# A hybrid decoder trunk: the compression of one attention branch as 16 joint products for keys and values

## The reference

```python
nc = S // CMP_STRIDE - 1                       # 256 // 16 - 1 = 15
def compress(t, pe, w):                        # t: (B, S, 64), pe: (32, 64), w: (32 * 64, 64)
    ch = t.reshape(B, S // CMP_STRIDE, CMP_STRIDE, d)
    blk = jnp.concatenate([ch[:, :-1], ch[:, 1:]], axis=2)
    return ((blk + pe).reshape(B, nc, CMP_LEN * d) @ w).astype(F32)
kc = compress(keys[:, :, 0], cmp_pe[0], w_cmp[0])
vc = compress(vals[:, :, 0], cmp_pe[1], w_cmp[1])
```

## Time and profile before

| | |
|---|---|
| median of 3 timed runs | 1626.65 us (1624.82 to 1626.75) |
| profiled execution | 1623.64 us, span 1622.0 us |
| TensorE busy | 1543.1 us (95%) |
| VectorE busy | 1250.4 us (77%) |
| ScalarE busy | 1015.1 us (63%) |
| mean granted TensorE clock | 0.961 of full |
| mixer of layer 0, loop and transposes | about 80 to 156 us |
| mixer of layer 1, loop and transposes | about 503 to 581 us |
| experts | from about 625 us to the end |

### The profile page before, as it was taken

How to read it: one execution, slowest core, us unless ns; L and a number is a source line. 1 busy time by engine, 2 the same in 40 slices (tenths; PEclk the granted TensorE clock), 3 DMA queues, 4 the chain that set the end, 5 groups by cost and what they waited for, 6 DMA issues and landing times.

```text
span 1622.0 us, 20490 instructions
## 1 busy us (share of the span) xinstructions
PE 1543.1 (95%) x7534; PEld 1293.3 (80%) x7534; DVE 1250.4 (77%) x1279; ACT 1015.1 (63%) x920; POOL 77.8 (5%) x106
## 2 busy tenths in 40 slices
PE   7989899999799995999999999999999999999996
PEld 5978688888698874888888888888888888888884
DVE  6777654444558666889988988988988988988985
ACT  6456443444355442778778778778778778777763
POOL 2101000000000011000000000000000000000000
PEclk9988999999899695999999999999999999999998
DMA  9701555556350032999999999999999999999991
GB/s 299 230 1 38 188 196 190 182 182 196 105 191 27 1 104 92 381 393 350 384 393 349 387 393 346 394 394 343 395 395 343 393 396 342 393 397 352 393 397 40
DMA packets 189879, 444.69 MB, mean 274 GB/s; under 512 B 9633, under 2 KB 15918, under 8 KB 189822
## 3 DMA queue, kind: packets, MB, share of 16 engines
q1 hardware_dynamic: 185214, 427.82, 71.8%
q0 software_dynamic: 4608, 16.10, 3.9%
HBM read 436.03 MB, written 7.86 MB: 274 GB/s over the span
## 4 chain that ended last, share of the span: by engine, by line
PE 91%; DVE 5%; issue 2%; ACT 1%; DMA 0%; POOL 0%; SPq 0%; ACTq 0%; POOLq 0%; DVEq 0%
PE bank L408 26%; PE bank L409 25%; PE bank L407 25%; PE bank L535 2%; PE bank L462 2%; PE bank L538 1%; PE bank L674 1%; PE bank L656 1%; PE bank L633 1%; DVE work L1737 1%; PE bank L684 1%; DVE hT L1557 1%; PE bank L648 1%; PE bank L863 0%; PE bank L387 0%
## 5 line engine op out<-in xcount | busy, mean ns | idle before, releaser
L1602 DVE TENSOR_TENSOR w_lo<-ring,w_hi 128x2048 fp32r<-128x2048 f32 x375 | 853.5, 2291 | 193.6 <-ACT w_hi L1211 192.2
L1211 ACT ACTIVATE w_hi<-ring 128x2048 fp32r<-128x2048 f32 x375 | 716.1, 1915 | 222.0 <-PE bank L407 221.9
L408 PE MATMUL bank<-w_hi,xT_hi 128*128 128x512 f32 x896 | 354.5, 396 | 5.8 <-ACT w_hi L1211 5.8
L409 PE MATMUL bank<-w_hi,xT_lo 128*128 128x512 f32 x896 | 350.5, 391 | 0.0
L407 PE MATMUL bank<-w_lo,xT_hi 128*128 128x512 f32 x896 | 240.6, 390 | 0.0
L408 PE MATMUL bank<-w_hi,hidT_hi 128*128 128x512 f32 x560 | 220.5, 394 | 1.6 <-DVE hidT_lo L1609 1.6
L409 PE MATMUL bank<-w_hi,hidT_lo 128*128 128x512 f32 x560 | 218.3, 390 | 0.0
L408 PEld LDWEIGHTS bank<-w_hi,xT_hi 128*128 128x128 f32 x896 | 168.9, 188 | 40.2 <-ACT w_hi L1211 6.2
L407 PEld LDWEIGHTS bank<-w_lo,xT_hi 128*128 128x128 f32 x896 | 168.7, 188 | 35.7
L409 PEld LDWEIGHTS bank<-w_hi,xT_lo 128*128 128x128 f32 x896 | 169.0, 189 | 34.0
L408 PE MATMUL bank<-w_hi,hT_hi 128*128 128x512 f32 (+2 forms) x384 | 149.8, 393 | 9.9 <-DVE hT_lo L1562 9.8
(11 more groups left out here) (335 smaller groups left out, 1395.0 us busy)
## 6 DMA issues: line engine op xcount, KB each, us to landing
ring<-in_moe_w_gate_dram SPq DMA_DIRECT2D x112, 1024.0 KB, 9.9
ring<-in_moe_w_up_dram SPq DMA_DIRECT2D x112, 1024.0 KB, 9.3
ring<-in_moe_w_down_dram SPq DMA_DIRECT2D x112, 1024.0 KB, 9.5
ring<-in_ffn_w_gate_dram SPq DMA_DIRECT2D x14, 1024.0 KB, 5.2
ring<-in_ffn_w_up_dram SPq DMA_DIRECT2D x14, 1024.0 KB, 5.1
ring<-in_ffn_w_down_dram SPq DMA_DIRECT2D x14, 1024.0 KB, 4.9
ring<-in_w_in_dram SPq DMA_DIRECT2D x12, 1024.0 KB, 5.2
ring<-in_w_out_dram SPq DMA_DIRECT2D x8, 1024.0 KB, 7.4
```

The lines of the kernel that those rows point to most:

```text
L408: pe.matmul(o, x_hi, w, start=start, stop=False)
L409: return pe.matmul(o, x_lo, w, start=False, stop=False)
L1211: act.activation(w_hi[:, (base + at) % SPLIT, :], ring[:, i, :], ACT.Copy).then_inc(hi_ready, 1)
L1602: dve.tensor_tensor(w_lo[:, v, :], ring[:, (base + at) % RING, :], w_hi[:, v, :].bitcast(F32), ALU.subtract).then_inc(lo_ready, 1)
```

## The change

The 32 positions of a block are split into two halves of 16. The raw keys and values are turned twice, into partitions 0 to 63 and again into 64 to 127, side by side as `kvT2`. Partitions 0 to 63 then serve positions 0 to 15 and partitions 64 to 127 positions 16 to 31. The lower copy is a transpose as before, the upper one a plain product with the identity. The weights of keys and values lie beside each other, 128 columns in 128 rows, and 16 products of 128 rows, 128 columns and 30 streamed columns (15 blocks of keys, 15 of values) give both results at once. Of the result, keys by keys' columns (rows 0 to 63) and values by values' columns (rows 64 to 127) are used. Values come out turned and are transposed once more (`turn_values`).

```diff
-        w_cmp = sb("w_cmp", [P, CLEN, HD])
-        pe_row = sb("pe_row", [CLEN, L, P])
-        pe_t = sb("pe_t", [P, L, CLEN])
+        w_cmp = sb("w_cmp", [P, CLEN // 2, 2 * HD])
+        pe_t = sb("pe_t", [P, L, 2, CLEN // 2])
...
+        pe_row = work[0:CLEN // 2, out_at + TB * GW:out_at + 2 * TB * GW].rearrange("p (l c q) -> p l c q", l=L, c=2)
...
-        N_PROW = 12
+        N_PROW = 13
...
             for l in range(L):
-                mm = pe.transpose(b[:, 2 * P + l * CLEN:2 * P + (l + 1) * CLEN], pe_row[:, l, :],
-                                  ident[0:CLEN, 0:CLEN])
+                for c in range(2):
+                    at = 2 * P + (2 * l + c) * (CLEN // 2)
+                    mm = pe.transpose(b[:, at:at + CLEN // 2], pe_row[:, l, c, :], ident[0:CLEN // 2, 0:CLEN // 2])
...
-                    pe.wait_ge(mixw_in, 64 * (l + 1))
+                    pe.wait_ge(mixw_in, 96 * (l + 1))
...
                 b = bank(1)
-                for tb in range(TB):
-                    pe.transpose(b[:, tb * P:(tb + 1) * P], utok[:, tb, KV0:KV0 + 2 * HD], ident[:, :])
-                for tb in range(TB):
-                    mm = pe.transpose(b[0:HD, S + tb * P:S + (tb + 1) * P],
-                                      utok[:, tb, KV0 + 2 * HD:KV0 + 3 * HD], ident[:, :])
+                for c in range(2):
+                    for tb in range(TB):
+                        v = utok[:, tb, KV0 + c * HD:KV0 + (c + 1) * HD]
+                        t = slice(c * S + tb * P, c * S + (tb + 1) * P)
+                        pe.transpose(b[0:HD, t], v, ident[:, :])
+                        mm = pe.matmul(b[HD:P, t], v, ident[:, :], start=True, stop=True)
                 give(mm, 1)
                 b = bank(1)
-                for tb in range(TB):
-                    mm = pe.transpose(b[0:HD, tb * P:(tb + 1) * P],
-                                      utok[:, tb, KV0 + 4 * HD:KV0 + 5 * HD], ident[:, :])
+                for i in range(2):
+                    for tb in range(TB):
+                        mm = pe.transpose(b[0:HD, i * S + tb * P:i * S + (tb + 1) * P],
+                                          utok[:, tb, KV0 + (2 + 2 * i) * HD:KV0 + (3 + 2 * i) * HD], ident[:, :])
...
-                def compressed_keys():
+                def compress():
 
                     pe.wait_ge(cin_ready, l + 1)
                     b = bank(0)
-                    for j in range(CLEN):
-                        mm = pe.matmul(b[0:HD, 0:NC], w_cmp[0:HD, j, :], cin[0:HD, j, :], start=(j == 0),
-                                       stop=(j == CLEN - 1))
+                    for j in range(CLEN // 2):
+                        mm = pe.matmul(b[:, 0:2 * NC], w_cmp[:, j, :], cin[:, j, :, :].rearrange("p c n -> p (c n)"),
+                                       start=(j == 0), stop=(j == CLEN // 2 - 1))
                     give(mm, 0)
+                    mark["cmp", l] = gave[0]
 
-                def compressed_values():
+                def turn_values():
 
+                    pe.wait_ge(cmp_ready, 2 * l + 1)
                     b = bank(0)
-                    for j in range(CLEN):
-                        mm = pe.matmul(b[0:NC, 0:HD], cin[HD:P, j, :], w_cmp[HD:P, j, :], start=(j == 0),
-                                       stop=(j == CLEN - 1))
-                    give(mm, 0)
-                    mark["cmp", l] = gave[0]
+                    give(pe.transpose(b[0:NC, 0:HD], kcv[HD:P, 1, :], ident[HD:P, HD:P]), 0)
...
                     if n == 3:
                         ssd_sums()
-                        compressed_keys()
+                        compress()
...
                     if n == 6:
-                        compressed_values()
+                        turn_values()
                         ssd_products()
...
-            sp.dma_start(pe_row[:, :, :].rearrange("r l (i d) -> r (l i) d", i=2),
-                         nsa_cmp_pe.rearrange("l i r d -> r (l i) d")).then_inc(prow_in, 16)
+            for half in range(2):
+                sp.dma_start(pe_row[:, :, :, half * HD:(half + 1) * HD].rearrange("r l c d -> r (l c) d"),
+                             nsa_cmp_pe[:, :, half * (CLEN // 2):(half + 1) * (CLEN // 2), :]
+                             .rearrange("l c r d -> r (l c) d")).then_inc(prow_in, 16)
...
-                for i in range(2):
-                    pool.dma_start(w_cmp[i * HD:(i + 1) * HD, :, :],
-                                   nsa_w_cmp[l, i].rearrange("(j d) e -> d j e", d=HD)).then_inc(mixw_in, 16)
+                for c in range(2):
+                    for half in range(2):
+                        pool.dma_start(w_cmp[half * HD:(half + 1) * HD, :, c * HD:(c + 1) * HD],
+                                       nsa_w_cmp[l, c, half * (CLEN // 2) * HD:(half + 1) * (CLEN // 2) * HD]
+                                       .rearrange("(j d) e -> d j e", d=HD)).then_inc(mixw_in, 16)
...
                 b = filled()
-                act.activation(kvcT[:, :], b[:, 0:S], ACT.Copy)
-                act.activation(ksT[0:HD, :], b[0:HD, S:2 * S], ACT.Copy).then_inc(act_took, 1)
+                act.activation(kvT2[:, :, :], b[:, :].rearrange("p (c t) -> p c t", c=2), ACT.Copy)\
+                    .then_inc(act_took, 1)
                 b = filled()
-                act.activation(kwT[0:HD, :], b[0:HD, 0:S], ACT.Copy).then_inc(act_took, 1)
+                act.activation(kswT[0:HD, :, :], b[0:HD, :].rearrange("p (c t) -> p c t", c=2), ACT.Copy)\
+                    .then_inc(act_took, 1)
...
-                for i in range(2):
-                    src = kvcT[:, 16 * i:16 * i + 16 * NC].rearrange("p (n j) -> p j n", j=16)
-                    pos = pe_t[:, l, 16 * i:16 * i + 16].unsqueeze(2).broadcast_to([P, 16, NC])
-                    ins = dve.tensor_tensor(cin[:, 16 * i:16 * i + 16, :], src, pos, ALU.add)
-                    if i == 0:
+                for half in range(2):
+                    r = slice(half * HD, (half + 1) * HD)
+                    at = half * (CLEN // 2)
+                    src = kvT2[r, :, at:at + 16 * NC].rearrange("p c (n j) -> p j c n", j=16)
+                    pos = pe_t[r, l, :, :].rearrange("p c j -> p j c").unsqueeze(3)\
+                        .broadcast_to([HD, CLEN // 2, 2, NC])
+                    ins = dve.tensor_tensor(cin[r, :, :, :], src, pos, ALU.add)
+                    if half == 0:
...
-                        take_bank(dve.tensor_copy(kcT[0:HD, :], b[0:HD, 0:NC]))
+                        take_bank(dve.tensor_copy(kcv[:, :, :], b[:, 0:2 * NC].rearrange("p (c n) -> p c n", c=2)))
```

More of the change, by code:

```diff
@@ L186, in trunk @@
                 at(b3, MLA_H, S), take(MLA_H, S),
-                at(b4, NH, S), take(S), take(S), take(S), take(NC), take(HD), take(TB, SSD_H),
-                at(b5, CLEN, NC), take(TB, GW), take(TB, GW), take(SSD_H, P),
+                at(b4, NH, S), take(2, S), take(2, NC), take(HD), take(TB, SSD_H),
+                at(b5, CLEN // 2, 2, NC), take(TB, GW), take(TB, GW), take(SSD_H, P), at(used[0] - SSD_H * P, 2, S),
                 at(b6, SSD_H, S)))
@@ L495, in _ @@
                 p = BASE_MIX[l]
-                (qtok, kcat, vtok, xb, xbc, qT, kT, nqT, kvcT, ksT, kwT, kcT, vc, nacs, cin, xtok, xdt, dec1,
+                (qtok, kcat, vtok, xb, xbc, qT, kT, nqT, kswT, kcv, vc, nacs, cin, xtok, xdt, dec1, kvT2,
                  dec0) = mix_bufs[l]
@@ L629, in scores @@
                             q, k = {"mla": (qT[0:QK, h, t0:t1], kT[0:QK, h, 0:nk]),
-                                    "cmp": (nqT[0:HD, h, t0:t1], kcT[0:HD, :]),
-                                    "sel": (nqT[0:HD, h, t0:t1], ksT[0:HD, 0:nk]),
-                                    "win": (nqT[0:HD, h, t0:t1], kwT[0:HD, 0:nk])}[br]
+                                    "cmp": (nqT[0:HD, h, t0:t1], kcv[0:HD, 0, :]),
+                                    "sel": (nqT[0:HD, h, t0:t1], kswT[0:HD, 0, 0:nk]),
+                                    "win": (nqT[0:HD, h, t0:t1], kswT[0:HD, 1, 0:nk])}[br]
                             mm = pe.matmul(b[:, i * nk:(i + 1) * nk], q, k, start=True, stop=True)
@@ L1534, in _ @@
             link(dve.tensor_copy(par[:, :, :], b[:, 0:2 * P].rearrange("p (l c) -> p l c", l=L)))
-            take_bank(dve.tensor_copy(pe_t[:, :, :], b[:, 2 * P:2 * P + L * CLEN].rearrange("p (l c) -> p l c", l=L)))
+            take_bank(dve.tensor_copy(pe_t[:, :, :, :], b[:, 2 * P:2 * P + L * CLEN]
+                                      .rearrange("p (l c j) -> p l c j", l=L, c=2)))
             def lam_start():
```

6 lines of the change are left out of this document (3 added, 3 removed).

## The result

The changed kernel takes 1640.7 us (median of 4 runs, 1638.8 to 1641.4) against 1626.1 us, a ratio of 1.0089 (95% interval 1.0072 to 1.0107). It is 14.6 us slower, and 15.7 us over the forecast. Its profiled execution took 1641.41 us, span 1639.6, granted clock 0.947 where before had 0.961.

A forecast was written before the change was run, and what follows sets the result against it. TensorE was taken as the bound, the chain running through it for 91% of the span. Terms 0 (joint products) - 3.75 + 1.6 + 0.5 = -1.65 us, so 1626.65 becomes 1625.0 us; range 1619.5 to 1630.5.

The forecast's parts named there:

- The value products' term: Mixers: value products leave TensorE, 3.67 us a layer; 2.1 us in layer 0 and 1.65 in layer 1 arrive, -3.75 together.
- Rival D: Between value transpose and squares (L760) the clock falls; 1628.5 us for one layer, 1632 for both; chance 0.17.
- The transposes: Before first scores: bank takes 1.3 us, ScalarE waits 0.64 and copies 0.17 longer; +0.81 us a layer, +1.6 in all.
- (C): New transpose bank: each change of output half drains, 1.3 us a layer, 1627.6 us; transposes' bound +2.1; chance 0.09.
- The dense FFN and the experts are the same instructions: Outside the mixers: whatever a mixer gains or loses moves dense FFN and experts as a block.
- Joint products: Mixers' key products: 32 records at 111 ns, 3.6 us, against 64 at 58 ns, 3.7 us; taken as 0.
- VectorE's additions: Building the products' input: double the elements, 2.3 us for 1.16, hidden by the wait before the scores; cost 0.
- its wait at the outputs: VectorE's 1.05 us wait at L1939 in each layer's mixer goes when the value products go.
- GpSimd's four loads: Compression weights: four DMAs where two took 2.19 us, 1.1 us more, at most 2.2; hidden, cost 0.
- The start: Kernel start: one more DMA issue, +0.30 us, and four narrow transposes for two, +0.36; +0.5 taken, bounds 0.3 and 0.7.
- The offset: Profiled execution of 1623.64 us, 3.0 under the median 1626.65; a difference worked out from it was put on the median.

The follow-up runs named there:

- Grouping: Changed kernel with its four lower-half transposes first, then its four upper-half products: 1631.7 us, ratio 1.0038.
- The transposes alone: Kernel before with four pairs of an upper-half product and a transpose added in each layer: 1633.6 us, ratio 1.0047.
- The three later traces with before's mixers: Kernel before with 44 tiny TensorE products (1632.8 us), with 56 (1626.8 us), and with its overflow loop inside one condition (1623.2 us).
- the padded kernel at 224: Kernel before with 56 tiny TensorE products in the waits around 640 us, final code at position 224 of a 256-instruction block: 1626.8 us, ratio 1.0010.
- the four attempts to hold it: Eight dense products added: changed kernel at n=6, 1639.8 us; also halves grouped, 1633.5; also at n=4, 1637.3; kernel before at n=4, 1648.9.

## Why the prediction was wrong

1. **The value products' term, -3.75 us, is the step that failed in the mixers.** Its working took the clock of the trace before as given and only moved work inside it. Removing them alone costs 6.7 us. Rival D named the mechanism, the stretch between the value transpose and the squares, and had 0.17. Its layer-0 form is in the trace after (0.50 from 143 to 149). In layer 1 more happened than it said: low from 549 to 580, where before was low from 540 to 557 only and high to 575.
2. **The transposes, +1.6 us, are mis-sized.** They took 2.27 us for the bank and +1.96 us a layer to the first scores, 3.9 in all, which is (C)'s 2.1 a layer. Grouping shows 0.13 us for each change. The Trainium skill's rule on drains (TensorEngine Tiling (Array Packing), Key Properties), as the prediction applied it, made this free; the measurement decides against that reading. Whether the half or the change between transpose and plain product drains was not separated. ScalarE waited 1.62 us, not 0.64. The transposes alone, 2.3 us later a layer, also took clock: 7.3 us in all.
3. **What the sum has no term for: the end, 7.6 us.** "The dense FFN and the experts are the same instructions" is true and did not help: TensorE's program ahead of them is 336 instructions shorter, and the jumps behind them cost by place. The experts themselves took the same time (961.1 and 961.3 us).
4. **Joint products, 0.** Right by themselves (111 ns a record), 0.5 to 4 us dearer in the kernel.
5. **VectorE's additions** took 1.98 us (forecast 2.3), and it still waited 1.00 us for the scores behind them: hidden, as forecast. In layer 0 its wait at the outputs (L1939 of before) went as forecast; in layer 1 it is 2.76 us where the earlier trace rows has 1.05, since TensorE is slow there.
6. **GpSimd's four loads** took 3.29 us for 2.19: +1.1, hidden, as forecast. **The start** was forecast at +0.5. Its parts came (four narrow transposes 0.55 us for 0.36, one issue of 0.32 us more), but the landing was 0.4 us shorter (2.17 for 2.58), and over the traces of both forms the first head transposes begin anywhere from 79.1 to 80.6 us. That term can't be told from nothing.
7. **The offset.** The forecast moved a difference from an execution of 1623.64 us. The three later traces with before's mixers have 34 us at half level in layer 0 (mixer 73.6 to 75.1 us), not the 24 us of the one I read, so its layer 0 was a lucky one. But that does not explain its 3 us under the median: the padded kernel at 224 took 1623.80 us with 34 us at half there, among other things because its combining products took 3.71 us for 5.25.

The parts alone are +1.2 (joint), +7.3 (transposes), +6.7 (value products) and, at the bad place, +7.6 us; together 23 us, where the whole is 14.6. They don't add. I put that down to the one clock through which three of them work; no run takes two parts together to show it. What stays open is why the same mixer code finds the clock at full or half in different executions; no run here settles it, and none of the four attempts to hold it has a median below the kernel before's. The Trainium skill (TensorE: Matmul & The Clock Gate, What's actually happening) calls the gate's phase run-variable. The scatter agrees, 1620.9 to 1640.0 us for one kernel.

## What to carry to other kernels

Where the granted clock moves between its levels inside the stretch that is changed, a sum of durations from one trace is no forecast: removed work can cost more than it took, so take the clock's fall as the first case and look at more than one execution. Count the length of an engine's program as a part of a change when jumps over unused code lie behind it, and put several skipped bodies behind one condition. Group the transposes that go to one half of the output.

## What the runs showed of the hardware

- Three jumps over an unused body cost TensorE 2.1 to 2.5 us in twelve traces and 3.3 to 9.9 us in the four where the code stands at one place (176 instructions within a 16 KB block, counted from before); with one jump it was 0.2 to 0.3 us. The two longest have four instruction transfers of 16 KB in the wait where the others have one.
- Changes between a lower-half transpose and an upper-half product cost 0.13 us each (six fewer, 2.27 to 1.47 us).
- The value products, 64 records of 15 weight and 64 streamed columns, ran at full clock in the traces before (3.67 us); without them the stretch from 142 to 159 us was at half. Put where the clock was low, they took 6.93 us and did not raise it. Eight products of 128x256, 3.5 us at full clock, did not replace them in the median.
- TensorE can be at half clock while its records fill the stretch: 17.00 of 17.00 us busy at 0.50.
